# A transfer cut in two, squares and roundings moved between VectorE and ScalarE, and first products reordered by kind

## The reference

```python
h = rms_norm(x, mix_norm_g[layer])
proj = h @ w_in[layer]
xr, yg, q, k, v = jnp.split(proj, splits, axis=-1)
...
x = x + mixed @ w_out[layer]
hf = rms_norm(x, ffn_norm_g[layer])
up = causal_depthwise_conv(hf @ w_up[layer], ffn_conv_w[layer], ffn_conv_b[layer])
gate, val = jnp.split(up, 2, axis=-1)
x = x + (jax.nn.gelu(gate) * val) @ w_down[layer]
```

## Time and profile before

| | |
|---|---|
| median of 3 runs | 292.92 us (292.85 to 292.94) |
| the profiled execution's own time | 292.89 us |
| its span | 291.1 us |
| TensorE busy | 285.6 us (98%) |
| VectorE busy | 243.7 us (84%) |
| ScalarE busy | 202.8 us (70%) |
| granted clock of TensorE | 1.00 throughout |
| transfers | 52.23 MB, mean 179 GB/s |

### The profile page before, as it was taken

How to read it: one execution, slowest core, us unless ns; L and a number is a source line. 1 busy time by engine, 2 the same in 40 slices (tenths; PEclk the granted TensorE clock), 3 DMA queues, 4 the chain that set the end, 5 groups by cost and what they waited for, 6 DMA issues and landing times.

```text
span 291.1 us, 5011 instructions
## 1 busy us (share of the span) xinstructions
PE 285.6 (98%) x1646; PEld 247.1 (85%) x1646; DVE 243.7 (84%) x448; ACT 202.8 (70%) x382; POOL 11.9 (4%) x28
## 2 busy tenths in 40 slices
PE   7999999999999999999999999999999999999996
PEld 6688999998788999888888888888888888888885
DVE  2998898889999768999977888888788888888875
ACT  4794599999875589787767666667676666676540
POOL 4000005500000000000000000000000000000000
PEclk9999999999999999999999999999999999999999
DMA  7999940431374703374738455454637444200003
GB/s 282 422 424 419 394 172 0 146 144 29 126 266 160 272 18 146 144 288 155 279 145 289 146 195 186 156 200 147 270 144 267 165 162 172 98 0 0 0 0 144
DMA packets 8111, 52.23 MB, mean 179 GB/s; under 512 B 928, under 2 KB 1312, under 8 KB 2080
## 3 DMA queue, kind: packets, MB, share of 16 engines
q1 hardware_dynamic: 7920, 51.50, 47.3%
q0 software_dynamic: 176, 0.53, 0.5%
HBM read 50.98 MB, written 1.05 MB: 179 GB/s over the span
## 4 chain that ended last, share of the span: by engine, by line
PE 93%; DMA 2%; DVE 2%; ACT 1%; SPq 0%; issue 0%; ACTq 0%
PE bank L1393 26%; PE bank L1046 15%; PE bank L1047 14%; PE bank L1050 14%; PE bank L1397 14%; PE bank L1102 3%; DMA x_tok<-in_x_dram 2%; PE bank L1166 1%; PE bank L1296 1%; PE bank L1197 1%; PE bank L1368 1%; DVE h_both L948 1%; PE bank L1360 1%; PE bank L1206 1%; PE bank L1160 1%; PE bank L1330 0%
## 5 line engine op out<-in xcount | busy, mean ns | idle before, releaser
L689 DVE TENSOR_TENSOR w_lo<-raw,w_hi 128x1024 fp32r<-128x1024 f32 x94 | 112.1, 1219 | 5.4 <-ACT w_hi L375 4.6
L375 ACT ACTIVATE w_hi<-raw 128x1024 fp32r<-128x1024 f32 x85 | 86.3, 1059 | 2.7 <-PE bank L1050 2.3
L1393 PE MATMUL bank<-h_both,w_hi 128*128 128x512 f32 x336 | 83.7, 391 | 0.0
L1393 PEld LDWEIGHTS bank<-h_both,w_hi 128*128 128x128 f32 x336 | 61.6, 188 | 11.8
L1397 PEld LDWEIGHTS bank<-h_both,w_lo 128*128 128x128 f32 x336 | 45.8, 190 | 3.3
L1397 PE MATMUL bank<-h_both,w_lo 128*128 128x256 f32 x336 | 46.8, 282 | 0.0
L604 ACT ACTIVATE tanh_a<-bank 128x256 f32<-128x256 f32 x44 | 16.8, 382 | 40.3 <-PE bank L1397 40.1
L1047 PE MATMUL bank<-w_lo,act_hi 128*128 128x512 f32 (+1 forms) x90 | 34.8, 387 | 0.0
L1046 PE MATMUL bank<-w_hi,act_hi 128*128 128x512 f32 (+1 forms) x90 | 34.8, 387 | 0.0
L1050 PE MATMUL bank<-w_hi,act_lo 128*128 128x512 f32 (+1 forms) x90 | 34.6, 384 | 0.0
L612 ACT ACTIVATE xc<-ygate,par 128x256 f32<-128x256 f32 x44 | 26.2, 595 | 3.6 <-DVE ygate L971 3.6
(11 more groups left out here) (188 smaller groups left out, 397.5 us busy)
## 6 DMA issues: line engine op xcount, KB each, us to landing
raw<-in_stream_dram SPq DMA_DIRECT2D x47, 1024.0 KB, 4.8
x_tok<-in_x_dram SPq DMA_DIRECT2D x2, 512.0 KB, 5.0
out_dram<-x_tok SPq DMA_DIRECT2D x3, 256.0 KB, 2.1
p_T<-in_gates_dram POOLq DMA_DIRECT2D x1, 512.0 KB, 9.4
out_dram<-x_tok SPq DMA_DIRECT2D x2, 128.0 KB, 2.0
par<-in_params_dram SPq DMA_DIRECT2D x1, 117.0 KB, 6.6
mix_g<-in_params_dram POOLq DMA_DIRECT2D x1, 4.0 KB, 5.6
```

The source lines that it names most:

```text
L375: act.activation(w_hi[u % RING][:, :], raw_unit(u), ACT.Copy).then_inc(hi_done, 1)
L689: dve.tensor_tensor(w_lo[u % RING][:, :], raw_unit(u), w_hi[u % RING][:, :].bitcast(F32), ALU.subtract).then_inc(lo_done, 1)
L1393: pe.matmul(acc[:, :], whi[:, kc, :], h_both[:, kc, :, :].rearrange("p b t -> p (b t)"), start=kc == 0, stop=False)
```

## The change

The transfer of raw[0] is cut in two, with x1's transfer between the halves; unit 0 has a semaphore of its own, on which q_plain and ScalarE's hi(0) wait. All squares of x1 go from ScalarE to one instruction of VectorE with a semaphore of its own, x_sum. VectorE's order in the opening becomes: half the squares of x0, reciprocal and scaling of x0, squares of x1, hi(1), reciprocal and scaling of x1, h_lo of (0,2) and (0,3), lo(1), lo(0), and on as before. Units 0 and 2 are rounded by ScalarE: hi(0) right behind the scaling of x1, hi(2) behind eight h_hi, hi(3) behind four more, ahead of the two plain ones. TensorE's first_product goes away: the high products of (0,2) and (0,3) come ahead of x1's transposes, their low-h products behind, and their low-w products among those of x1.

```diff
-VECTOR_HI = (1, 0, 2, 17, 18, 20, 21, 19, 22)
+VECTOR_HI = (1, 17, 18, 20, 21, 19, 22)
...
             sp.dma_start(x_tok[:, 0, :], x_t[0]).then_inc(x_landed[0], 16)
-            sp.dma_start(raw[0][:, :], stream[0]).then_inc(raw_landed[0], 16)
+            sp.dma_start(raw[0][:, 0:UNIT], stream[0][:, 0:UNIT]).then_inc(unit0_landed, 16)
             sp.dma_start(x_tok[:, 1, :], x_t[1]).then_inc(x_landed[1], 16)
+            sp.dma_start(raw[0][:, UNIT:2 * UNIT], stream[0][:, UNIT:2 * UNIT]).then_inc(raw_landed[0], 16)
...
-            x_square(1, slice(0, 1024))
             x_root(1, eps)
             x_scale(1)
-            for at in HI_ORDER[2:14]:
+            hi(0)
+            for at in HI_ORDER[2:10]:
                 h_part(*at)
+            hi(2)
+            for at in HI_ORDER[10:14]:
+                h_part(*at)
+            hi(3)
             plain_hi(0)
             plain_hi(1)
-            his(3)
...
+            def x_square_all():
+                dve.wait_ge(x_landed[1], 16)
+                dve.tensor_tensor_reduce(flat(tanh_a), x_tok[:, 1, :], x_tok[:, 1, :], 1.0, 0.0, ALU.mult,
+                                         ALU.add, x_ss[:, 1:2]).then_inc(x_sum, 1)
...
             x_reciprocal(0)
             x_scale(0)
+            x_square_all()
             hi(1)
-            los(1)
+            x_reciprocal(1)
+            x_scale(1)
             h_part(0, 2)
             h_part(0, 3)
-            x_reciprocal(1)
-            x_scale(1)
-            hi(0)
-            hi(2)
+            los(1)
             los(0)
...
-            first_product(0, 2)
-            first_product(0, 3)
+            early, later = ((0, 2), (0, 3)), ((1, 0), (1, 1), (1, 2), (1, 3))
+            q_high(early)
             transpose_x(1)
-            q_by_kind(((1, 0), (1, 1), (1, 2), (1, 3))).then_inc(unit_used, 2)
+            q_low_h(early)
+            q_high(later)
+            q_low_w(early + later)
+            q_low_h(later).then_inc(unit_used, 2)
             for u in (2, 3):
-                q_by_kind(((0, 2 * u), (0, 2 * u + 1), (1, 2 * u), (1, 2 * u + 1))).then_inc(unit_used, 1)
+                both = ((0, 2 * u), (0, 2 * u + 1), (1, 2 * u), (1, 2 * u + 1))
+                q_high(both)
+                q_low_w(both)
+                q_low_h(both).then_inc(unit_used, 1)
```

More of the change, by code:

```diff
@@ L186, in build_layer @@
         raw_landed = [sem(f"raw_landed{r}") for r in range(RAW)]
+        unit0_landed = sem("unit0_landed")
         x_landed = [sem(f"x_landed{m}") for m in range(TT)]
@@ L195, in build_layer @@
         plain_done = sem("plain_done")
-        x_sq, x_mean_done = sem("x_sq"), sem("x_mean_done")
+        x_sq, x_sum, x_mean_done = sem("x_sq"), sem("x_sum"), sem("x_mean_done")
         own_hi, q_scale_done, f_added = sem("own_hi"), sem("q_scale_done"), sem("f_added")
@@ L370, in hi @@
             def hi(u, it=None):
-                act.wait_ge(raw_landed[(u // 2) % RAW], at_pass(it, 16, 16 * (u // 2 // RAW + 1)))
+                if u == 0:
+                    act.wait_ge(unit0_landed, 16)
+                else:
+                    act.wait_ge(raw_landed[(u // 2) % RAW], at_pass(it, 16, 16 * (u // 2 // RAW + 1)))
                 if u >= RING:
@@ L390, in x_root @@
             def x_root(m, bias):
-                act.wait_ge(x_sq, m + 1)
+                act.wait_ge((x_sq, x_sum)[m], 1)
                 act.activation(x_rms[:, m:m + 1], x_ss[:, m:m + 1], ACT.Sqrt, bias=bias,
@@ L703, in x_scale, with x_square_half @@
                                   ALU.mult).then_inc(x_normed[m], 1)
-            def x_square(m):
-                dve.wait_ge(x_landed[m], 16)
-                half = x_tok[:, m, 0:512]
+            def x_square_half():
+                dve.wait_ge(x_landed[0], 16)
+                half = x_tok[:, 0, 0:512]
                 link(dve.tensor_tensor_reduce(flat(tanh_a)[:, 0:512], half, half, 1.0, 0.0, ALU.mult,
@@ L724, in _ @@
             dve.memset(ones[:, :], 1.0).then_inc(ones_done, 1)
-            x_square(0)
+            x_square_half()
             x_reciprocal(0)
             x_scale(0)
+            x_square_all()
             hi(1)
-            los(1)
+            x_reciprocal(1)
+            x_scale(1)
             h_part(0, 2)
             h_part(0, 3)
-            x_reciprocal(1)
-            x_scale(1)
-            hi(0)
-            hi(2)
+            los(1)
             los(0)
@@ L1071, in rows_product @@
                              w_hi[u % RING][:, cols], w_lo[u % RING][:, cols], kc == 0, kc == KC - 1)
[L1073 to L1082, removed]
             def rows_unit(u, first_unit, banks):
@@ L1092, in q_plain @@
             def q_plain(kc):
-                pe.wait_ge(raw_landed[0], 16)
+                pe.wait_ge(unit0_landed, 16)
                 pe.wait_ge(plain_done, kc + 1)
@@ L1102, in q_part, with q_high @@
                 return pe.matmul(Q_ACC[m][:, :], h_part[:, kc, tok], w_part[at][:, cols], start=first, stop=last)
-            def q_by_kind(parts):
+            def q_high(parts):
                 for m, kc in parts:
@@ L1113, in q_by_kind, with q_low_w @@
                     q_part(m, kc, h_hi, w_hi, first=(m, kc) == (1, 0))
+            def q_low_w(parts):
                 for m, kc in sorted(parts, key=lambda at: lo_count(U_Q + at[1] // 2)):
@@ L1116, in q_by_kind, with q_low_h @@
                     q_part(m, kc, h_hi, w_lo)
+            def q_low_h(parts):
                 for m, kc in sorted(parts, key=LO_ORDER.index):
```

## The result

The changed kernel takes 293.92 us (median of 6 runs, 293.76 to 294.28) where the kernel before takes 292.90 (292.67 to 292.95): ratio 1.0036, 95% interval 1.0026 to 1.0046. It is 1.0 us slower; I had said 292.65, and a range that ended at 293.1. The profiled execution took 293.86 us, its span 292.1.

The account below looks back on a forecast made before the run. TensorE, busy 98%, bounds the kernel, leaving the opening: transposes 0.88 us earlier, minus 0.91 for moved matmuls, plus 0.11 and 0.17 of removed idling, gain 0.25. From 292.92 to 292.67, given as 292.65; range 292.25 to 293.1.

Parts of the forecast that it names:

- the one on the transfers: Opening's queue: with x1 between the weight halves, x1 lands at 7.24 instead of 8.50 and unit 1 at 8.50.
- The dip at 5 us: Transfer rate in the opening: a dip tied to a time, 5.0 to 6.5 us, that both kernels pass through.
- my bounds: Unit 1's landing in the opening: 7.83 at 416 GB/s, 8.83 at 329, 9.26 at 302; 8.50 taken.
- first sign of being wrong: Opening, VectorE: squares of x1 starting after 7.6 would show the transfers wrong; forecast start 7.26.
- The third rival: Opening, VectorE: unit 1 landing after 8.50 delays x1's reciprocal; 293.0 at 8.83, 293.4 at 9.26; chance 0.13.
- Squares on VectorE, 1.23 us by a line through two widths: Opening: x1's squares on VectorE take 1.23 us, from 7.26 to 8.49; this step alone loses 0.07 us.
- hi(1) in front of the reciprocal: Opening, VectorE: rounding unit 1 first, 8.53 to 9.22, delays x1's reciprocal and gives back 0.3 us of the gain.
- Four products behind the transposes: Opening, TensorE: four matmuls moved behind x1's transposes take 0.91 us off the 0.88 us earlier transposes.
- hi(0), hi(2), hi(3) on ScalarE cost nothing: Opening, ScalarE: casts at 0.98 us each stay hidden; hi(0)'s 0.14 is covered, lo(2) keeps 0.35 us slack.
- q_plain at 7.40 whatever unit 0 does: Opening, TensorE: q_plain still starts at 7.40, behind the first transposes, with the gain vector landing at 6.87.
- The lead is carried to the end: After the opening: the 0.25 us gain is carried on by TensorE, busy without a break until far behind.
- The Trainium skill's rule of 1 MiB or more per transfer: Opening's transfers: about 2.0 us fixed cost each would, if in line, make the kernel 5 us slower; judged to overlap.

Follow-up runs that it names:

- e1: Changed kernel with the first weight block laid out so each half transfer reads contiguous memory; 292.95 us, ratio 1.0001 against before.
- e7: e1 with x1 transferred ahead of all weights, its reciprocal and scaling ahead of hi(1), its transposes ahead of the early pair; 292.80 us, ratio 0.9991.
- e10: e7 without the gain vector's transfer, the vector set to 1.0 on the chip; 292.81 us.
- e3: Changed kernel with the first weight transfer whole again and x1 behind it, compute orders as changed; 293.63 us, ratio 1.0024.
- e11: e7 with the gain vector's transfer issued on ScalarE's queue instead of GpSimd's; 292.37 us, ratio 0.9981.
- e12: e1 with the gain vector's transfer issued by ScalarE at its start instead of by GpSimd; 292.63 us, ratio 1.0003.
- e9: Kernel before with second to fourth weight transfers cut into strided halves, all three first halves issued before the three second ones; 298.39 us.
- e5: Kernel before with second to fourth weight transfers each cut into two strided halves, issued one behind the other; 293.48 us.

## Why the prediction was wrong

The step that failed is the one on the transfers: "By bytes x1 takes the old place of units 0+1 (1.57 MB moved), 7.24, and unit 1 the old place of x1, 8.50." They landed at 8.52 and 9.80. I had priced the cut at nothing but 0.43 us of issue, and taken the rate from rows in which no transfer skipped memory; the half transfers read 4 KB out of every 8 KB, and the first of them ran at 205 to 229 GB/s for 3 us. The dip at 5 us that I had tied to a time does stay there in e1, e7 and e10, with 271 to 287 GB/s from 5.0 to 5.5; the strided read has a deeper one of its own, which began at 3.5 us. None of my bounds held it: the lowest, 302 GB/s, was the lowest of a kernel without such a read, and an end of the range has to come from the nearest operation, or be called unknown and be wide. The prediction's first sign of being wrong, squares of x1 after 7.6, was met at 8.54; a result above 293.51 had a chance of 0.07.

The third rival (unit 1's landing holds VectorE in front of the reciprocal) came nearest: its rule gives 292.67 + (9.80 - 8.50) = 293.97, and 293.92 was measured. It had chance 0.13 and a price that stopped at 293.4. But its number is better than its mechanism, and that is luck: it had x1 on time and unit 1 alone late, whereas x1 was late by 1.28 and unit 1 by 1.30. The squares of the late x1 would have held VectorE until 9.7 anyway: in e3, where unit 1 had landed long before, hi(1) starts at 9.69 instead of 9.82.

The other steps:

- *Squares on VectorE, 1.23 us by a line through two widths.* Right: 1.23.
- *hi(1) in front of the reciprocal.* Right in kind; the square root was ready at 10.11, the reciprocal started at 10.43, 0.3 given away as worked out.
- *Four products behind the transposes.* Right in size: the low-h row is 3.78 behind the transposes' start (15.07 - 11.29), where before it was 3.19 (14.09 - 10.90), 0.6 more; forecast 0.63.
- *hi(0), hi(2), hi(3) on ScalarE cost nothing.* Right: lo(2) waited 0.23 us for hi(2), and TensorE showed no wait for it.
- *q_plain at 7.40 whatever unit 0 does.* Wrong by 0.38 (7.78): the gain vector landed at 7.25 instead of 6.87, in the slow stretch. It was hidden, since TensorE then waited for hi(1) until 10.57.
- *The lead is carried to the end.* The changed kernel had none to carry; the leads of e10, e11 and e12 (13.30 to 13.81 against 14.09) arrive whole, and the losses too, by the table of thirteen executions.
- *The Trainium skill's rule of 1 MiB or more per transfer* ("DMA: Bandwidth & Descriptors", Rules for kernel authors). I set it aside, as the trace did not show a fixed cost in line, and that stands: in e11 and e12 transfers of 512 KB ran at 393 to 434 GB/s from 3.5 to 7.0 us. It was the stride inside the halves that cost, not their size. The 2.0 us of fixed cost that the prediction sets beside the rule are fitted on that page, in Anatomy of one DMA, to transfers that GpSimd issues, and the halves are issued by SyncE; no run here measures them.

## What to carry to other kernels

A transfer cut in two is not the old transfer twice: look at what each half reads in memory, and lay the data out so that it is contiguous before the order of transfers is tuned. Before a reordering is priced by bytes, look at when the last of the 16 engines ends, as the landing is that. Where one engine is busy to the end, find the row from which it never waits again: here the time was that row's start plus 278.8 us in thirteen executions, and every experiment but e9 could be read off it.

## What I had not expected of the hardware

- The first transfers that read 4 KB of every 8 KB run at 205 to 260 GB/s for 1 to 3 us, at 3.5 us or at 8.5 us of the kernel; later ones hold 401 GB/s or more (e5, e9). The 4 KB packets then have a median of 248 to 260 ns instead of 159. Its cause is open; whether it depends on the amount read before wasn't tried.
- Moving one transfer of 4 KB from GpSimd's queue to ScalarE's took the spread of e7's runs from 1.03 us (292.01 to 293.04) to 0.21 (292.26 to 292.47), and its dip from 5 to 2.5 us, while dropping that transfer did not (e10: 0.93). So it is not the small descriptors themselves; whether it is the second queue in use early on is open. It isn't a rule either: the same move in e12 left two of eleven runs 1.2 us and more behind the rest. The Trainium skill ("DMA: Bandwidth & Descriptors", Rules for kernel authors) says that spreading transfers over queues gives no bandwidth, only issue time. The traces agree: from 1.5 to 6.5 us e7 moved 1.56 MB and e11 1.63, and both run at 410 GB/s from 10.0 to 10.5. The evenness of the sixteen ends, in which the two profiled executions differ (unit 0's within 1.83 us in e7, 0.38 in e11), is another matter.
